# One layer of a hybrid encoder on one core: tiles scaled as rows before they are turned, roots spread later, gains fetched as rows, row tiles stored ahead of h rows

## The chip, the core and the metric

The kernel is one program on one core of a Trainium2 chip. The metric is the time on the device in microseconds (us); the median of three runs of the kernel before is 2344.55 us (2340.38 to 2346.22). The engines are TensorE (PE in the profile), VectorE (DVE), ScalarE (ACT), GpSimd (POOL) and SyncE (SP). SP and GpSimd issue nearly all transfers, and each issues in program order: a transfer whose condition is not met holds up all that stand behind it on that engine.

## The reference

One step of a layer on 1024 prompt tokens and 32 sample tokens, all in fp32. What matters here:

```python
n = rmsnorm(h, g_in)            # x * rsqrt(mean(x*x) + eps) * g_in, per token
z = n @ w_in                    # 2048 -> 6152: q, k, v, f, gates, u
att = forgetting_attention(q, k, v, f)
ssm = s5(u)                     # diagonal state space, GELU, GLU
mixed = concat(att * silu(ga), ssm * silu(gs))
h = h + mixed @ w_out           # the residual is the input x
e = rmsnorm(pe @ w_pe, g_pe)
h = h + e * sigmoid(h @ w_pg)
y = rmsnorm(h, g_final)
```

The outputs are y, k, v, the log of the forget gates and the last states, for prompt and sample.

## The kernel before, in words

Activations are held transposed, features on the 128 partitions and the 1056 tokens along the free axis. The three large products (`w_in`, `w_out`, `w_pg`) are made by a seven-product scheme (Winograd's form of Strassen's): features and tokens are cut in halves, giving seven "sides" (sums and differences of quarter blocks of the activations) and seven weight factors. Each fp32 operand is split into a high and a low part, so a product of one side is 4 feature tiles x 3 combinations x 2 token quarters = 24 matmuls of 264 columns. A *pair* `p` is 256 output columns in one half of the sum; its seven products `r` = 0 to 6 go to three pairs of PSUM banks (X, B, Y). ScalarE makes the high part of each weight factor (`high`) and copies banks, DVE makes the factor sums and low parts (`sums`, `low`) and adds partial results. All engines follow the same double loop, `p` and slot `j`, written out by hand: what stands in slot `j` of a pair on DVE or ScalarE runs in that order and waits on semaphores.

`stage_front` (L196) begins with a prologue. For each of ten token tiles (two halves of 4 x 128 + 16 tokens) SP loads `x_in` (rows of 2048). ScalarE squares and sums the row (`square`), takes the root (`root`) and, after PE has turned the first 1024 features (`turn_x`), copies the turned tile over the first half of `x_in` (`copy_x`), from where SP stores it to `xT` in DRAM, for the residual. DVE makes the reciprocal and a diagonal matrix `x_dg` of it (`spread`); PE multiplies that by ones (L711), which lays the reciprocals of the tile's tokens on every partition; DVE copies them to `rstd_bc` and multiplies the eight turned feature tiles by gain and reciprocal into `n_raw` (`normalize`, L1216). After tile 5's root the first two sides are cast and subtracted (`high_side`, `low_side`); for tiles 5 to 9 DVE also makes four differences (`sub_tiles`). The gain comes by columns, `g_col`, one element per descriptor. The other 1024 features follow during pairs 0 to 5 (`turn_xb`, `copy_xb`, `ride`) and read `rstd_bc`.

`stage_attention` and `stage_side` are not touched. `stage_mix` (L2592) has four groups of eight pairs (`NPM` = 8): pairs 0 to 7 and 8 to 15 for `w_out`, 16 to 23 and 24 to 31 for `w_pg`. Between groups all seven sides are replaced: GpSimd reloads each (`reload_side`), ScalarE casts it, DVE subtracts. Four of the seven sides are made ahead from row tiles, the *ride*: GpSimd loads a ride tile (`load_ride`), DVE makes four differences in slot 6 (`subtract_rides`), GpSimd stores them to `tS` (`store_ride`) and, once all have landed, loads the next tile. The ride for group 2 runs in pairs 11 to 15, beside the part loads (`load_part`) and the stores of h rows (`store_h`) of pairs 8 to 15. SP loads weights, the residual (`load_residual`, into `x_res`), and in pairs 2 to 6 (`E_AT`) one block of e each, which DVE scales in slot 5 by `g_pe` and the reciprocals (`scale_e`, L3242) and SP stores back. In slot 6 follows `c12` (L3227), for which PE's product 1 of the next pair waits.

GpSimd's order in pairs 8 to 15 is this:

```python
for n in range(4):
    if NPM + KEPT <= p + 1 < 2 * NPM and n < 3:
        load_part(p + 1, n)
    if p > NPM:
        store_h(p - 1, n)
if 1 <= r <= NRIDE:
    store_ride(2, r - 1)
if 0 <= r < NRIDE:
    load_ride(2, r)
```

## Time and profile before

| | |
|---|---|
| runs | 2344.55 us median (2340.38 to 2346.22, n = 3) |
| profiled execution | 2348.45 us; its span, first to last instruction, 2346.6 us |
| busy, share of the span | PE 92%, DVE 71%, ACT 43%, POOL 13% |
| mean granted TensorE clock | 0.966 of full speed |
| DMA | 477.63 MB, mean 204 GB/s |
| stretches (us from the start) | prologue to 62.8, rest of the front stage to about 1066, attention to about 1460, side stage to about 1582, mixing stage to the end |

All times in rows are from the start of the span. "Idle before" is how long the engine stood ahead of an instruction, and after the arrow is what ended it. A row with xN is N instructions in one stretch. SPq and POOL rows of DMA are the issue of a transfer, not its landing.

### The profile page before, as it was taken

The page shows a single profiled execution, that of the slowest core. Times are in us where ns is not written, and L with a number is a line of the kernel's source. Part 1 is how long each engine was busy: PE and PEld are TensorE (multiplying, and loading weights), DVE is VectorE, ACT ScalarE, POOL GpSimd, SP SyncE. Part 2 cuts the span into 40 slices and gives each one's busy share as a digit, 9 for nine tenths or more (in the row PEclk, how much of TensorE's full clock was granted, in tenths as well). Part 3 has the DMA queues.
Part 4 walks back from the last instruction along what each step waited for, and adds up shares of the span by engine and source line. Part 5 has one row for each costly group of instructions (what it writes and reads, how often), then busy time and mean ns, then how long its engine had stood idle before and what let it go on. Part 6 is the DMA issues. An engine that isn't in the chain of part 4 may idle for free. (4 is left out here: it accounts for less than half of the span.)

```text
span 2346.6 us, 44727 instructions
## 1 busy us (share of the span) xinstructions
PE 2167.0 (92%) x16739; PEld 2107.7 (90%) x16739; DVE 1656.2 (71%) x3053; ACT 999.1 (43%) x1863; POOL 307.5 (13%) x459
## 2 busy tenths in 40 slices
PE   3999999999999999999979988988899998999994
PEld 3999999999999999999958867988899998999994
DVE  6779767767786878787536655758667657658775
ACT  6443333333533333334457645324235324335554
POOL 0021000000101111111144320000101221101000
PEclk7999999999999999999989998999999999999997
DMA  8484444444557787877367735454766677857578
GB/s 249 136 269 119 144 128 138 140 129 145 197 171 226 217 232 219 229 217 207 106 210 237 234 111 218 147 178 175 274 238 228 228 272 253 302 174 253 212 253 326
DMA packets 328006, 477.63 MB, mean 204 GB/s; under 512 B 78912, under 2 KB 250280, under 8 KB 318016
## 3 DMA queue, kind: packets, MB, share of 16 engines
q1 hardware_dynamic: 265072, 290.58, 39.8%
q0 software_dynamic: 36976, 139.52, 17.3%
q10 hardware_dynamic: 25760, 44.87, 5.9%
q8 instruction: 127, 2.08, 0.4%
q14 instruction: 71, 0.58, 0.1%
HBM read 295.99 MB, written 170.22 MB: 199 GB/s over the span
## 5 line engine op out<-in xcount | busy, mean ns | idle before, releaser
L757 PE MATMUL acc<-t_act,w_hi 128*128 128x264 f32 x5376 | 888.1, 287 | 9.2 <-DVE zb L1319 7.3
L757 PEld LDWEIGHTS acc<-t_act,w_hi 128*128 128x128 f32 x5376 | 748.9, 189 | 15.6 <-issue 14.2
L2937 PE MATMUL m_acc<-m_t_act,m_hi 128*128 128x264 f32 x3584 | 597.6, 289 | 38.2 <-DVE m_zb L3227 9.6
L757 PE MATMUL acc<-t_act,w_lo 128*128 128x264 f32 x2688 | 548.5, 286 | 0.0
L2937 PEld LDWEIGHTS m_acc<-m_t_act,m_hi 128*128 128x128 f32 x3584 | 506.2, 192 | 42.6 <-issue 28.3
L757 PEld LDWEIGHTS acc<-t_act,w_lo 128*128 128x128 f32 x2688 | 417.8, 189 | 0.0
L2937 PE MATMUL m_acc<-m_t_act,m_lo 128*128 128x264 f32 x1792 | 369.2, 288 | 0.0
L1312 DVE TENSOR_TENSOR w_lo<-w_raw_f,w_hi 128x512 fp32r<-128x512 f32 x288 | 198.0, 687 | 136.0 <-ACT w_hi L967 135.7
L967 ACT CAST w_hi<-w_raw_f 128x512 fp32r<-128x512 f32 x288 | 177.9, 618 | 268.6 <-PE acc L757 240.1
L2937 PEld LDWEIGHTS m_acc<-m_t_act,m_lo 128*128 128x128 f32 x1792 | 282.1, 192 | 0.0
L2986 ACT CAST m_hi<-m_raw 128x512 fp32r<-128x512 f32 x192 | 118.7, 620 | 166.3 <-PE m_acc L2937 125.4
L3199 DVE TENSOR_TENSOR m_lo<-m_raw,m_hi 128x512 fp32r<-128x512 f32 x192 | 131.8, 687 | 65.8 <-ACT m_hi L2986 65.8
L651 POOL DMA_DIRECT2D zT<-zb x80 | 43.3, 543 | 341.1 <-DVE zb L1328 142.5
L2244 DVE CUSTOM_DVE_ANT_0 prob<-score,negc_bc 128x128 f32<-128x128 f32 (+8 forms) x72 | 53.4, 750 | 30.2 <-PE score L2017 28.9
L1016 ACT COPY zb<-acc 128x528 f32<-128x528 f32 x40 | 24.0, 600 | 116.4 <-PE acc L757 116.4
L2268 DVE TENSOR_TENSOR pt_lo<-turned,pt_hi 128x512 fp32r<-128x512 f32 (+2 forms) x112 | 52.8, 507 | 27.2 <-ACT pt_hi L2160 25.4
L2149 ACT ACTIVATE prob<-prob,stat 128x128 f32<-128x128 f32 (+8 forms) x72 | 56.1, 781 | 21.7 <-DVE stat L2244 14.8
L665 POOL DMA_DIRECT2D zb<-cT x88 | 47.3, 540 | 131.4 <-issue 54.2
L984 ACT COPY acc<-acc 128x528 f32<-128x528 f32 x48 | 28.0, 583 | 67.8 <-PE acc L757 64.0
L640 POOL DMA_DIRECT2D t_act<-tS x7 | 3.7, 534 | 403.0 <-PE acc L757 403.0
L3153 DVE TENSOR_TENSOR m_t_act<-m_t_act 128x2112 fp32r<-128x2112 f32 x23 | 54.1, 2352 | 0.0
L1312 DVE TENSOR_TENSOR w_lo<-s,w_hi 128x512 fp32r<-128x512 f32 x48 | 33.2, 691 | 25.6 <-ACT w_hi L967 25.6
(429 smaller groups left out, 3391.6 us busy)
## 6 DMA issues: line engine op xcount, KB each, us to landing
w_raw_f<-in_w_in_dram SPq DMA_DIRECT2D x96, 512.0 KB, 3.9
cT<-zb SPq DMA_DIRECT2D x22, 1056.0 KB, 4.2
zb<-cT POOLq DMA_DIRECT2D x88, 264.0 KB, 6.2
zT<-zb POOLq DMA_DIRECT2D x80, 264.0 KB, 4.0
m_e_res<-eT SPq DMA_DIRECT2D x16, 1056.0 KB, 9.6
m_raw<-in_w_out_dram SPq DMA_DIRECT2D x32, 512.0 KB, 6.2
m_raw<-in_w_pg_dram SPq DMA_DIRECT2D x32, 512.0 KB, 6.1
cT<-m_zb SPq DMA_DIRECT2D x12, 1056.0 KB, 5.1
```

What stands on the lines that cost most here:

```text
L651: pool.dma_start(d["zT"][row:row + P, tok:tok + HN], zb[b][:, i]).then_inc(z_put[i], 16)
L665: pool.dma_start(zb[b][:, i], d["cT"][p - NP][:, i]).then_inc(z_got[i], 16)
L757: mm = pe.matmul(out[:, c, 0:QN], w[:, k, :], t_act[:, SIDE[r], x, k, c * QN:(c + 1) * QN], start=(opens and k == 0 and m == 0), stop=(k = ...
L967: nc.scalar.copy(w_hi[n % RING_W][:], factor(p, r)).then_inc(hi_done, 1)
L1312: TT_(w_lo[n % RING_W][:], factor(n // 7, n % 7), w_hi[n % RING_W][:].bitcast(F32), ALU.subtract) \
L2149: e = nc.scalar.activation(prob[s % 4][:, col:col + width], prob[s % 4][:, col:col + width], ACT.Exp, scale=-1.0, bias=stat[b][:, n, 0:1], ...
L2244: z = nc.vector.tensor_tensor_reduce(out=prob[s % 4][:, col:col + width], in0=score[b][:, col:col + width], in1=negc[hb][:, row:row + widt ...
L2268: c = nc.vector.tensor_tensor(out, src, hi.bitcast(F32), ALU.subtract)
L2937: mm = pe.matmul(out[:, c, 0:QN], w[:, k, :], t_act[:, MSIDE[r], x, k, c * QN:(c + 1) * QN], start=(opens and k == 0 and m == 0), stop=(k ...
L2986: nc.scalar.copy(w_hi[n % RING_W][:], factor(p, r)).then_inc(hi_done, 1)
L3153: TT_(t_act[:, MSIDE[s], 1], raw, t_act[:, MSIDE[s], 0].bitcast(F32), ALU.subtract) \
L3199: TT_(w_lo[n % RING_W][:], factor(n // 7, n % 7), w_hi[n % RING_W][:].bitcast(F32), ALU.subtract) \
```

## The change

In the prologue DVE scales the first 1024 features of each tile as rows (`scale_rows`, into `x_rows`), PE turns these too (`turn_rows`), and `normalize` multiplies the turned rows from PSUM by the gain in two operations; so `x_dg`, the matrix of ones and the copy per tile go, and the raw tile is still turned and copied for the residual. The reciprocals are laid out for all tokens by ten matmuls within pair 0 (`spread`) and four ScalarE copies (`copy_bc`). A root is taken ahead of the first square. `copy_x` of a tile follows the next tile's root. The cast and subtraction of side 1 go ahead of weight factors 1 and 2. Both gains (`g_in`, `g_pe`) are loaded as 16 rows of 128 and turned by PE; the second in pair 2 of the mixing stage ahead of product 4. The residual blocks of pairs 8 and 9 are loaded in pairs 3 and 5 rather than both in pair 2. GpSimd stores the ride tiles ahead of part loads and h rows, and reloads sides 1 to 3 between the h rows of pair 14.

```diff
@@ stage_front: PE @@
-            def spread(t):
+            def turn_rows(t):
                 rows = TILES[t][1]
-                pe.wait_ge(dg_done, t + 1)
-                if t >= 2:
-                    pe.wait_ge(bc_copied, t - 1)
-                pe.matmul(oth[:, t % 2, 0:rows], ones[0:rows, :], dg[t % 2][0:rows, 0:rows], start=True, stop=True) \
-                    .then_inc(bc_done, 1)
+                pe.wait_ge(rows_scaled, t + 1)
+                for h in range(2):
+                    if t:
+                        pe.wait_ge(n_half, 2 * (t - 1) + h + 1)
+                    for f in range(KQ):
+                        tr = pe.transpose(acc[:, 4 + h, f * P:f * P + rows],
+                                          x_rows[t % 2][0:rows, (h * KQ + f) * P:(h * KQ + f + 1) * P],
+                                          ident[0:rows, 0:rows])
+                    tr.then_inc(rows_turned, 1)
+            def spread(bank, tiles):
+                pe.wait_ge(rstd_done, max(tiles) + 1)
+                for n, t in enumerate(tiles):
+                    rows = TILES[t][1]
+                    mm = pe.matmul(oth[:, bank, n * rows:(n + 1) * rows], stat[0:rows, t, 2:3].to_broadcast([rows, P]),
+                                   ident[0:rows, 0:rows], start=True, stop=True)
+                mm.then_inc(bc_done, 1)
...
+            turn_x(0)
+            pe.wait_ge(g_loaded, 16)
+            pe.transpose(oth[:, 0, 0:KD], rstd_bc[0:KD, 0:P], ident[0:KD, 0:KD]).then_inc(g_turned, 1)
             for t in range(10):
-                turn_x(t)
-                spread(t)
+                if t < 9:
+                    turn_x(t + 1)
+                turn_rows(t)
...
+                    if p == 0 and r == 3:
+                        spread(0, (0, 1, 2, 3))
+                        spread(1, (5, 6, 7, 8))
+                    if p == 0 and r == 5:
+                        pe.wait_ge(bc_copied, 1)
+                        spread(0, (4, 9))
@@ stage_front: ScalarE @@
+            nc.scalar.activation(stat[:, 0, 3:4], eps[:], ACT.Sqrt)
             for t in range(10):
                 square(t)
                 root(t)
-                copy_x(t)
+                if t:
+                    copy_x(t - 1)
...
+            copy_x(9)
+            high(0)
+            act.wait_ge(t_sub, 5)
+            high_side(2, 1, side_raw[1])
+            for n in range(1, RING_W - 1):
                 high(n)
-            for i, s in ((2, 1), (3, 2)):
-                act.wait_ge(t_sub, 5)
-                high_side(i, s, side_raw[s])
+            high_side(3, 2, side_raw[2])
@@ stage_front: DVE @@
-            def spread(t):
+            def scale_rows(t):
                 dve.wait_ge(std_done, t + 1)
                 nc.vector.reciprocal(stat[0:rows, t, 2:3], stat[0:rows, t, 1:2]).then_inc(rstd_done, 1)
                 dve.wait_ge(rstd_done, t + 1)
                 if t >= 2:
-                    dve.wait_ge(bc_done, t - 1)
-                TS(dg[t % 2][0:rows, 0:rows], ident[0:rows, 0:rows], stat[0:rows, t, 2:3], None, ALU.mult) \
-                    .then_inc(dg_done, 1)
+                    dve.wait_ge(rows_turned, 2 * (t - 1))
+                TS(x_rows[t % 2][0:rows], x_in[t][0:rows, 0:D_MODEL // 2], stat[0:rows, t, 2:3], None, ALU.mult) \
+                    .then_inc(rows_scaled, 1)
...
-                for f in range(8):
-                    s = STT(n_raw[:, f // 4, f % 4, tok:tok + rows], x_t[t][:, f, 0:rows], g_col[:, f:f + 1],
-                            rstd_bc[:, tok:tok + rows], ALU.mult, ALU.mult)
-                s.then_inc(n_done, 1)
+                for h in range(2):
+                    dve.wait_ge(rows_turned, 2 * t + h + 1)
+                    TT_(n_raw[:, h, :, tok:tok + rows], acc[:, 4 + h].rearrange("p (f t) -> p f t", f=KQ)[:, :, 0:rows],
+                        g_col[:, h * KQ:(h + 1) * KQ].unsqueeze(2).to_broadcast([P, KQ, rows]), ALU.mult) \
+                        .then_inc(n_half, 1)
@@ stage_mix: SP @@
                 if p == 2:
                     sp.wait_ge(t_ready, 7)
-                    load_residual(NPM)
-                    load_residual(NPM + 1)
-                    with nc.allow_non_contiguous_dma("per-feature columns of the gain"):
-                        sp.dma_start(g_pe[:], d["g_pe"][0].rearrange("(k p) -> p k", p=P)).then_inc(gains_loaded, 16)
+                    sp.dma_start(x_part[0][0:KD, 0:P], d["g_pe"][0].rearrange("(k p) -> k p", p=P)) \
+                        .then_inc(gains_loaded, 16)
+                if p in (3, 5):
+                    load_residual(NPM + (p - 3) // 2)
@@ stage_mix: GpSimd @@
             for p in range(NPM, 2 * NPM):
                 r = p - FIRST_RIDE[2]
+                if 1 <= r <= NRIDE:
+                    store_ride(2, r - 1)
                 if p == 2 * NPM - 1:
                     reload_side(2, 0)
...
                         store_h(p - 1, n)
-                if 1 <= r <= NRIDE:
-                    store_ride(2, r - 1)
+                    if p == 2 * NPM - 1 and n > 0:
+                        reload_side(2, n)
                 if 0 <= r < NRIDE:
                     load_ride(2, r)
-            for s in range(1, 7):
+            for s in range(4, 7):
                 reload_side(2, s)
@@ stage_mix: PE @@
+                    if p == 2 and r == 4:
+                        pe.wait_ge(gains_loaded, 16)
+                        pe.transpose(oth[:, 0, 0:KD], x_part[0][0:KD, 0:P], ident[0:KD, 0:KD]).then_inc(gains_turned, 1)
@@ stage_mix: DVE, scale_e @@
-                dve.wait_ge(gains_loaded, 16)
+                if n == 0:
+                    dve.wait_ge(gains_turned, 1)
+                    link(nc.vector.tensor_copy(g_pe[:], oth[:, 0, 0:KD]))
```

DVE, prologue, tile 6 with the second tile of differences. Before (`x_in_59` is tile 6; the diagonal made in its first two rows is tile 7's):

```order
L1199 RECIPROCAL x_stat<-x_stat 128x1
L1203 TENSOR_SCALAR x_dg_66<-ident,x_stat 128x128
L1209 COPY rstd_bc<-oth 128x128
L1216 SCALAR_TENSOR_TENSOR n_raw<-x_in_59,g_col,rstd_bc 128x128 x8
L1227 TENSOR_TENSOR zb<-n_raw 128x4x128
L1228 TENSOR_TENSOR zb<-n_raw,zb 128x4x128
L1229 TENSOR_TENSOR n_raw<-n_raw 128x4x128
L1230 TENSOR_TENSOR n_raw<-n_raw,zb 128x4x128
```

And now (the first two rows scale tile 7's rows, `x_in_60`):

```order
L1240 RECIPROCAL x_stat<-x_stat 128x1
L1244 TENSOR_SCALAR x_rows_66<-x_in_60,x_stat 128x1024
L1251 TENSOR_TENSOR n_raw<-acc,g_col 128x4x128 x2
L1262 TENSOR_TENSOR zb<-n_raw 128x4x128
L1263 TENSOR_TENSOR zb<-n_raw,zb 128x4x128
L1264 TENSOR_TENSOR n_raw<-n_raw 128x4x128
L1265 TENSOR_TENSOR n_raw<-n_raw,zb 128x4x128
```

Ten operations on 128 tokens and the copy have become one of 1024 and two of 512 elements; the four differences stay.

SP, mixing stage, pair 2 and the start of pair 3. Before:

```order
L2770 DMA cT<-m_zb 128x2112
L2742 DMA m_raw_21072<-in_w_out_dram 128x4x256
L2755 DMA m_x_res<-xT 128x2x1056 x2
L2777 DMA m_g_pe<-in_g_pe_dram 128x16x1
L2758 DMA m_e_res<-eT 128x2x1056
L2742 DMA m_raw_21073<-in_w_out_dram 128x4x256
L2806 DMA eT<-m_e_res 128x2x1056
```

And now, to the e block of pair 3:

```order
L2805 DMA cT<-m_zb 128x2112
L2777 DMA m_raw_21109<-in_w_out_dram 128x4x256
L2809 DMA m_x_part_22080<-in_g_pe_dram 16x128
L2793 DMA m_e_res<-eT 128x2x1056
L2777 DMA m_raw_21110<-in_w_out_dram 128x4x256
L2841 DMA eT<-m_e_res 128x2x1056
L2805 DMA cT<-m_zb 128x2112
L2777 DMA m_raw_21108<-in_w_out_dram 128x4x256
L2790 DMA m_x_res<-xT 128x2x1056
L2793 DMA m_e_res<-eT 128x2x1056
```

The two residuals have left their place ahead of pair 2's e block; one now stands ahead of pair 3's.

GpSimd, end of pair 14 and pair 15, where the sides for group 2 are reloaded. Before:

```order
L2860 DMA m_ride<-hT 128x1056 x2
L2831 DMA m_t_act<-hT 128x4x528
L2840 DMA hT<-m_x_res 128x528 x4
L2867 DMA tS<-m_ride 128x528 x4
L2831 DMA m_t_act<-tS 128x2112 x2
L2831 DMA m_t_act<-hT 128x4x528
L2831 DMA m_t_act<-tS 128x2112
```

And now:

```order
L2895 DMA m_ride<-hT 128x1056 x2
L2902 DMA tS<-m_ride 128x528 x4
L2866 DMA m_t_act<-hT 128x4x528
L2875 DMA hT<-m_x_res 128x528 x2
L2866 DMA m_t_act<-tS 128x2112
L2875 DMA hT<-m_x_res 128x528
L2866 DMA m_t_act<-tS 128x2112
L2875 DMA hT<-m_x_res 128x528
L2866 DMA m_t_act<-hT 128x4x528
```

The last row tiles have moved ahead of the first reload and of the h rows, and the reloads stand between the h rows.

## Rows read from the trace of the kernel before

**Rows 1.** The page, busy time of the engines (share of the span, instructions)

```profile
PE 2167.0 (92%) x16739; PEld 2107.7 (90%) x16739; DVE 1656.2 (71%) x3053; ACT 999.1 (43%) x1863; POOL 307.5 (13%) x459
```

**Rows 2.** Waits of PE: engine, line, for whom, total us, times, longest

```profile
PE m_acc L2937 <- DVE m_zb L3227: 9.6, 1, 9.6
```

**Rows 3.** Timeline, ScalarE, prologue: start us, us, instruction [idle before]

```profile
6.04 1.28 ACT L907 ACT_TABLE_LOAD   x1 [6.04 <-DMA x_in<-in_x_prompt_dram]
...
9.35 1.28 ACT L913 ACT_TABLE_LOAD   x1
...
11.79 1.92 ACT L907 ACTIVATE x_sq<-x_in 128x2048 f32<-128x2048 f32 x1
...
15.11 1.92 ACT L907 ACTIVATE x_sq<-x_in 128x2048 f32<-128x2048 f32 x1
...
30.23 3.95 ACT L933 CAST t_act<-n_raw 128x2112 fp32r<-128x2112 f32 x2
```

**Rows 4.** Timeline, DVE, second half of the prologue

```profile
42.56 0.29 DVE L1203 TENSOR_SCALAR x_dg<-ident,x_stat 128x128 f32<-128x128 f32 x1
...
43.08 2.19 DVE L1216 SCALAR_TENSOR_TENSOR n_raw<-x_in,g_col,rstd_bc 128x128 f32<-128x128 f32 x8
45.30 0.69 DVE L1227 TENSOR_TENSOR zb<-n_raw 128x512 f32<-128x512 f32 x1
...
48.16 0.29 DVE L1203 TENSOR_SCALAR x_dg<-ident,x_stat 128x128 f32<-128x128 f32 x1
```

**Rows 5.** Timeline, PE, prologue and first product

```profile
29.88 1.47 PE L701 MATMUL acc<-ident,x_in 128*128 128x128 f32 x8
...
62.87 0.78 PE L752 MATMUL acc<-t_act,w_hi 128*128 128x264 f32 x2 [8.24 <-issue]
```

**Rows 6.** Groups of DVE instructions by line and shape: count, busy us, mean ns

```profile
L3363 DVE TENSOR_SCALAR m_y_out<-m_y_all,m_rstd 128x2048 f32<-128x2048 f32 x5 | 6.2, 1282 | 0.5 <-DMA m_y_all<-yS 0.5
...
L3153 DVE TENSOR_TENSOR m_t_act<-m_t_act 128x2112 fp32r<-128x2112 f32 x23 | 54.1, 2352 | 0.0
```

**Rows 7.** Timeline, PE, four fp32 matmuls between products

```profile
770.36 1.06 PE L851 MATMUL oth<-u_in,ws_in 128*128 128x132 f32 x8
```

**Rows 8.** Timeline, SP, ScalarE, DVE and PE, mixing stage, pair 2

```profile
1645.40 2.31 SPq L2755 DMA_DIRECT2D m_x_res<-xT  x2
...
1648.33 12.14 SPq L2758 DMA_DIRECT2D m_e_res<-eT  x1
...
1646.63 0.60 ACT L3021 COPY m_zb<-m_acc 128x528 f32<-128x528 f32 x1 [1.81 <-PE m_acc L2937]
...
1651.74 0.69 DVE L3181 TENSOR_TENSOR m_raw<-m_raw,m_raw 128x512 f32<-128x512 f32 x1 [2.74 <-DMA m_raw<-in_w_out_dram]
...
1667.55 2.55 DVE L3242 SCALAR_TENSOR_TENSOR m_e_res<-m_e_res,m_g_pe,e_rstd 128x1056 f32<-128x1056 f32 x2 [12.70 <-DMA m_e_res<-eT]
1670.02 0.70 DVE L3227 TENSOR_TENSOR m_zb<-m_acc,m_zb 128x528 f32<-128x528 f32 x1
...
1670.87 1.22 PE L2937 MATMUL m_acc<-m_t_act,m_hi 128*128 128x264 f32 x4 [9.58 <-DVE m_zb L3227]
```

**Rows 9.** Stretches: busy us (instructions) of PE, PEld, DVE, ACT, POOL, clock, DMA share, GB/s

```profile
1650.00:1655.00 5.00, 5.00 (x43) 5.00 (x42) 3.12 (x5) 1.31 (x3) 0.84 (x2) 1.00 1.04 386
...
1670.00:1675.00 5.00, 4.13 (x19) 4.17 (x20) 4.97 (x8) 0.62 (x1) 0.00 (x0) 0.50 0.55 220
...
1900.00:1950.00 50.00, 45.09 (x359) 43.94 (x358) 34.11 (x53) 15.82 (x25) 13.64 (x25) 1.00 0.81 282
```

**Rows 10.** Timeline, GpSimd and PE, the crossings at pairs 7 and 15

```profile
1789.78 1.22 PE L2937 MATMUL m_acc<-m_t_act,m_hi 128*128 128x264 f32 x4 [3.94 <-DVE m_zb L3206]
...
1928.40 1.14 POOL L2860 DMA_DIRECT2D m_ride<-hT  x2 [8.10 <-DMA tS<-m_ride]
...
1950.30 1.07 POOL L2831 DMA_DIRECT2D m_t_act<-tS  x2 [5.48 <-DMA tS<-m_ride]
...
1961.24 1.22 PE L2937 MATMUL m_acc<-m_t_act,m_hi 128*128 128x264 f32 x4 [6.77 <-issue]
```

More of the change, by code:

```diff
@@ L235, in stage_front @@
         n_raw = place("n_raw", [P, 2, KQ, T])
-        dg = [place(f"x_dg{b}", [P, P]) for b in range(2)]
+        x_rows = [nc.alloc_sbuf_tensor_at(f"x_rows{b}", [P, D_MODEL // 2], F32, offset=ring_at + 4 * D_MODEL + b * 2 * D_MODEL)
+                  for b in range(2)]
         blk = [[n_raw[:, kh, :, th * HN:(th + 1) * HN] for th in range(2)] for kh in range(2)]
@@ L304, in stage_front @@
         consts, g_loaded, arena_open = sem("consts"), sem("g_loaded"), sem("arena_open")
+        g_turned = sem("g_turned")
         x_loaded = [sem(f"x_loaded{t}") for t in range(10)]
-        x_squared, std_done, rstd_done, dg_done, bc_done, bc_copied, x_turned, x_copied, n_done = (
-            sem(n) for n in ("x_squared", "x_std_done", "x_rstd_done", "dg_done", "bc_done", "bc_copied",
-                             "x_turned", "x_copied", "n_done"))
+        x_squared, std_done, rstd_done, rows_scaled, rows_turned, bc_done, bc_copied, x_turned, x_copied, n_half = (
+            sem(n) for n in ("x_squared", "x_std_done", "x_rstd_done", "rows_scaled", "rows_turned", "bc_done",
+                             "bc_copied", "x_turned", "x_copied", "n_half"))
         xT_stored = [sem(f"xT_stored{t}") for t in range(5)]
@@ L717, in turn_xb @@
                     pe.wait_ge(xb_loaded, 16 * sum(len(list(x_pieces(t))) for i in range(m + 1) for t in (i, i + 5)))
+                if m == 0 and h == 0:
+                    pe.wait_ge(bc_copied, 3)
                 if m == 1 and h == 1:
@@ L1146, in extra, with copy_bc @@
                         nc.scalar.activation(sp_part, sp_part, ACT.Ln, bias=ones_col[0:HEADS, :]).then_inc(gate_ln, 1)
+            def copy_bc(n):
+                first, width, bank, at = ((0, 4 * P, 0, 0), (HN, 4 * P, 1, 0), (4 * P, 16, 0, 0), (HN + 4 * P, 16, 0, 16))[n]
+                act.wait_ge(bc_done, min(n, 2) + 1)
+                return nc.scalar.copy(rstd_bc[:, first:first + width], oth[:, bank, at:at + width])
             act.wait_ge(consts, 1)
+            nc.scalar.activation(stat[:, 0, 3:4], eps[:], ACT.Sqrt)
             for t in range(10):
@@ L1151, in _ @@
                 root(t)
-                copy_x(t)
+                if t:
+                    copy_x(t - 1)
                 if t == 5:
-                    act.wait_ge(n_done, 5)
+                    act.wait_ge(n_half, 10)
                     for i, s in enumerate(BUILD[:2]):
                         high_side(i, s, side_raw[s])
-            act.wait_ge(x_turned, 10)
-            for n in range(RING_W - 1):
+            copy_x(9)
[3 more added lines that the diff above has]
+            for n in range(1, RING_W - 1):
                 high(n)
-            for i, s in ((2, 1), (3, 2)):
-                act.wait_ge(t_sub, 5)
-                high_side(i, s, side_raw[s])
+            high_side(3, 2, side_raw[2])
             for p in range(2 * NP):
@@ L1179, in _ @@
                     high(7 * p + j + RING_W - 1)
+                    if p == 0 and j == 3:
+                        copy_bc(0).then_inc(bc_copied, 1)
+                        copy_bc(1).then_inc(bc_copied, 1)
+                    if p == 0 and j == 5:
+                        copy_bc(2)
+                        copy_bc(3).then_inc(bc_copied, 1)
                     if j == 1 and p > NP and is_silu(p - 1):
@@ L1240, in ride @@
                     dve.wait_ge(t_ready, 7)
+                    dve.wait_ge(bc_copied, 3)
                 if m and h == 0:
@@ L1713, in _ @@
             dve.wait_ge(consts, 1)
-            dve.wait_ge(g_loaded, 16)
+            dve.wait_ge(g_turned, 1)
+            link(nc.vector.tensor_copy(g_col[:], oth[:, 0, 0:KD]))
+            scale_rows(0)
             for t in range(5):
-                spread(t)
-                copy_bc(t)
+                scale_rows(t + 1)
                 normalize(t)
-            spread(5)
             for i, s in enumerate(BUILD[:2]):
@@ L1723, in _ @@
                 if t < 9:
-                    spread(t + 1)
-                copy_bc(t)
+                    scale_rows(t + 1)
                 normalize(t)
@@ L1730, in _ @@
             sums(2)
+            low_side(2, 1, side_raw[1])
             low(1)
             low(2)
-            for i, s in ((2, 1), (3, 2)):
-                low_side(i, s, side_raw[s])
+            low_side(3, 2, side_raw[2])
             for p in range(2 * NP):
@@ L2773, in _ @@
                     sp.wait_ge(t_ready, 7)
-                    load_residual(NPM)
-                    load_residual(NPM + 1)
-                    with nc.allow_non_contiguous_dma("per-feature columns of the gain"):
-                        sp.dma_start(g_pe[:], d["g_pe"][0].rearrange("(k p) -> p k", p=P)).then_inc(gains_loaded, 16)
+                    sp.dma_start(x_part[0][0:KD, 0:P], d["g_pe"][0].rearrange("(k p) -> k p", p=P)) \
+                        .then_inc(gains_loaded, 16)
+                if p in (3, 5):
+                    load_residual(NPM + (p - 3) // 2)
                 if p in E_AT:
```

28 lines of the change are left out of this document (11 added, 17 removed).

## Prediction

> **What bounds the kernel now.** I read the page first: TensorE (PE) is busy for 92% of the span [rows 1], so only the places where PE stands still are worth anything. The waits of PE, longest first, name them, and one entry lies in the stage this change edits: 9.6 us for DVE's `m_zb` [rows 2]. The order of time at each place then gives the cause. There are three.
>
> Prologue: PE's first product starts at 62.87 [rows 5], and all before it is preparation. ScalarE starts at 6.04 with a table load, pays a second at 9.35, and then takes one tile per 3.32 us (11.79 to 15.11); the first side is cast at 30.23 [rows 3]. In the second half DVE never rests: one tile takes 5.60 us (42.56 to 48.16), of which the eight `n_raw` operations take 2.22 and the four subtractions after 45.30 take 2.67 [rows 4].
>
> Pair 2 of the mixing stage (A): SP issues two residual blocks at 1645.40, then the gain by columns, and at 1648.33 the e block, whose issue alone lasts 12.14 us. DVE stands at that e block until 1667.55; behind it is the operation at 1670.02 that PE waits for; PE is idle for 9.58 us [rows 8]. The granted clock falls to 0.5, that is 1.2 instead of 2.4 GHz, after this idleness: 19 matmuls in 4.13 us, where a full window has 43 in 5.00 [rows 9].
>
> Pairs 11 to 16 (B): GpSimd sends the row tiles (`tS`) last, then stands at their landing before it loads the next (8.10 us at 1928.40); the sides are reloaded at 1950.30 only, and PE idles 6.77 us until 1961.24 [rows 10]. In 1900 to 1950, before that gap, 4.9 us are lost in small pieces [rows 9].
>
> **Prologue, part by part.** (1) The root's table is loaded while x travels, so the two loads of 1.28 us go: first root at about 8.4 instead of 10.9. (2) DVE scales whole rows: 128x1024 by a per-row scalar. The trace has 128x2048 of that form in 1282 ns [rows 6], so 0.65 us; the two-tensor form of 2,112 elements costs 2352 ns [rows 6], nearly twice as much per element, which would make it 1.1, the upper bound. (3) Eight STTs, one copy and one small scaling (2.22 + 0.32 + 0.20) become that 0.65 and two multiplications of 128x512 from PSUM; the nearest row has 128x528 in 0.70 us (at 1670.02) [rows 8], so 1.35. A second-half tile falls from 5.60 to about 4.85. (4) In the first half ScalarE's 3.32 us bounds: tile 5's root at about 23.9, then the last small tile's turn and multiplication, casts of the first sides from about 24.7 instead of 30.23: 5.5 earlier. (5) PE now turns each tile twice. Eight transposes take 1.92 us at the low clock, and two sets, 3.84, would exceed 3.32; but the set at 29.88 took 1.47 after PE had been busy since 27.27 [rows 5], so PE speeds up when it has this work. I take ScalarE's pace, and keep 2 us for PE's. (6) The casts and subtractions of the first two sides stay as they are; four full tiles save 0.75 each, the small one about 0.9. End of the prologue: 5.5 + 3.0 + 0.9 = 9.4 us earlier. (7) The roots are spread later, between PE-bound products: 8 + 2 fp32 matmuls. Four such of 132 columns show 1.06 us [rows 7], so 2.1, wholly on the path. The cast of side 1 is moved ahead of two weight casts; product 0 at the low clock lasts over 5 us and covers it, so I give it nothing (up to 0.5). The two ScalarE copies of 512 columns lie beside PE. Prologue net **-7.4**, from -4 (row scaling at 1.1, PE's pace) to -10.
>
> **A.** Residual blocks leave pair 2, and 2,048 elements by columns become 16 rows. The e block then has one store and one 512 KB weight block ahead of it rather than two residuals as well, and lands at about 1655; DVE scales it in 2.5 and does PE's operation by 1659, before PE needs it at 1661.3. So 9.58 and the low-clock loss (16 matmuls at 0.12 = 1.9) go: -11.5. Added: PE turns the gain ahead of pair 2's fifth product. Its third ended at 1646.63 (a copy waited for it) [rows 8], so the fifth starts at 1649.5; the rows of the gain stand behind the weight block which DVE gets at 1651.74: a new stop of 2.3 us (0 if the small load slips through, 4 if it is served late). Moved: a residual now stands ahead of the e block in pairs 3 and 5. 1.08 MB at 386 GB/s [rows 9] is 2.8 us later; the scaling and the operation behind it had some 2 us to spare there: 0.6. A: **-8.6**, from -12 to -5.
>
> **B.** Row tiles go ahead of the h rows, so they leave about 5 us earlier per pair, have landed when the next load is due, and the load goes 7 to 8 us earlier; DVE no longer stands at the ride. Most of the 4.9 goes: -4. At the crossing (pair 15) the last tiles leave near 1932 instead of 1942.7, and the reload of side 1 can go near 1939.5 instead of 1950.30. What is late next is DVE: seven side subtractions of 2.35 each [rows 6] on top of its usual work. The sister crossing at pair 7 has no late reload, and still shows 3.94 us at 1789.78 [rows 10] and the low clock behind it. So 6.77 becomes about 3.9, the restart stays half: -4.5. Side 0 now waits behind the four stores (6 us later), which its first use can just stand. B: **-8.5**; if the reloads simply fill the DMA engines -2, if the whole gap and clock loss go -14.
>
> Sum: 7.4 + 8.6 + 8.5 = 24.5. The profiled execution took 2348.45 (span 2346.6 and 1.85 around it), so 2324.0 for it; it lies 3.9 above the median of the runs, 2344.55, so **2320.0** as a median. Nothing else moves: stages between are shifted as a whole.
>
> **Rivals.** (R1) *The crossing does not improve* (0.17): side 0 is late behind the tile stores and DVE is the bound anyway; B gives 2 instead of 8.5: 2326.5. For it: the sister crossing. Against: 6.77 was a wait for landing, not for DVE.
> (R2) *DVE still stands at the e block* (0.10): with residuals ahead in pairs 3 and 5 it is late there, 3 us each with the operation behind it, and PE waits for the gain's rows: A gives 2.5: 2326.1. Against: pair 5 has no ride traffic.
> (R3) *Dearer table loads* (0.05): each load costs ScalarE a further emptying about as long as itself, so that two removed loads give 2.7 more and all first-half tiles shift: 2317.3. The row at 9.35 shows the next operation at once after 1.28, which speaks against it. The Trainium skill (ScalarE: Activation LUTs, What ACT_TABLE_LOAD costs) puts a drain of about 1.38 us beside the 1.28; the trace has no such gap ahead of the load.
> (R4) *The other side* (0.04): in pairs 12 to 15 GpSimd now stands at DVE's ride result first, with four part loads and four h stores queued behind; SP waits for the landing of all h rows before it loads a residual, and the next weight block queues behind it. It decides once h rows land more than about 8 us later; to lose the other gains each of four pairs must lose some 8 us: 4 x 8 - 16 = 16 slower: 2360. DVE had its result while GpSimd still held other work in every pair seen, hence the small chance.
> (R5) *No change* (0.05): the gains stand, but the freed transfers and the two extra residual slots return all but 4 us as small weight waits: 2341.
>
> **Numbers.** Forecast 0.59, R1 0.17, R2 0.10, R3 0.05, R4 0.04, R5 0.05. About 0.3% (7 us) is what a measurement can tell from no change. Faster by more: 0.59 + 0.17 + 0.10 + 0.05 = 0.91; same 0.05; slower 0.04. Worst ends together (4 + 5 + 2 = 11) give 2333.5, best (10 + 12 + 14 = 36) give 2308.5; both ends together are rare, and runs spread by some 3. Range 2309 to 2333.
>
> **What would show it.** Prologue: one table load before x lands, first product at 53 to 54, a DVE period near 4.9 in the second half, one stop or slow piece of 2 us in the first pair. A: a PE stop of about 2 us ahead of pair 2's fifth product for the gain, none of 9.6, granted clock 1.0 through the pair. B: no GpSimd wait for tile stores ahead of a ride load, side 1 reloaded within 11 us of pair 15's start, a gap of 3 to 5 us. It is wrong if the first product starts after 58, if DVE still waits over 5 us for an e block, or if the crossing keeps 6 us.

## The result and the profile after

The changed kernel takes 2323.79 us, median of 4 runs (2321.29 to 2324.04), against 2345.07 (2340.38 to 2346.22) for the kernel before, run beside it: a ratio of 0.9911, 95% interval 0.9893 to 0.9928. It is 21 us faster; 2320.0 was forecast, with a range of 2309 to 2333. The profiled execution took 2323.73, with a span of 2322.0 (before: 2346.6), so the two traces differ by 24.6 us, while the medians differ by 21.3: the traced execution of before lay 3.4 above its median. The page's first part, TensorE (PE) against [rows 1]:

```profile
PE 2167.6 (93%) x16821; PEld 2109.9 (91%) x16821; DVE 1650.5 (71%) x2985; ACT 1000.7 (43%) x1867; POOL 308.2 (13%) x458
```

The prologue, timeline of ScalarE (start, duration, in brackets the idle time before and what ended it), against [rows 3]:

```profile
0.87 1.28 ACT L1181 ACT_TABLE_LOAD   x1 [0.87 <-PEq L3504]
...
8.26 1.91 ACT L932 ACTIVATE x_sq<-x_in 128x2048 f32<-128x2048 f32 x1 [0.17 <-DMA x_in<-in_x_prompt_dram]
...
11.44 1.92 ACT L932 ACTIVATE x_sq<-x_in 128x2048 f32<-128x2048 f32 x1
...
24.60 3.94 ACT L959 CAST t_act<-n_raw 128x2112 fp32r<-128x2112 f32 x2 [1.07 <-DVE n_raw L1251]
```

One table load, before x is there; a tile every 3.18 us; the first sides are cast at 24.60 instead of 30.23, after a wait of 1.07 us for DVE. The second half on DVE, against [rows 4], has a period of 4.85:

```profile
31.32 0.76 DVE L1244 TENSOR_SCALAR x_rows<-x_in,x_stat 128x1024 f32<-128x1024 f32 x1
31.99 1.28 DVE L1251 TENSOR_TENSOR n_raw<-acc,g_col 128x512 f32<-128x512 f32 x2
...
36.17 0.75 DVE L1244 TENSOR_SCALAR x_rows<-x_in,x_stat 128x1024 f32<-128x1024 f32 x1
```

PE's first product, against 62.87 [rows 5], and the two root spreads that now stand between products:

```profile
53.14 0.78 PE L767 MATMUL acc<-t_act,w_hi 128*128 128x264 f32 x2 [4.71 <-issue]
...
63.58 1.95 PE L723 MATMUL oth<-ident,x_stat 128*128 128x128 f32 x16
...
71.33 0.61 PE L723 MATMUL oth<-ident,x_stat 16*128 16x16 f32 x4
```

Pair 2 of the mixing stage, timeline of SP's queue, PE and DVE, against [rows 8]:

```profile
1637.22 1.01 SPq L2809 DMA_DIRECT2D m_x_part<-in_g_pe_dram  x1
1638.60 0.76 SPq L2793 DMA_DIRECT2D m_e_res<-eT  x1
...
1643.53 0.29 PE L3003 MATMUL m_oth<-ident,m_x_part 16*128 16x16 f32 x1 [2.19 <-DMA m_x_part<-in_g_pe_dram]
...
1650.32 2.55 DVE L3284 SCALAR_TENSOR_TENSOR m_e_res<-m_e_res,m_g_pe,e_rstd 128x1056 f32<-128x1056 f32 x2
```

The e block's issue takes 0.76 us instead of 12.14 and DVE finds it landed, so the old stop of 9.58 us is gone. In its place PE stands 2.19 us for 16 rows of gain. Pair 3, which now has a residual block ahead of the e block:

```profile
1661.70 1.02 SPq L2790 DMA_DIRECT2D m_x_res<-xT  x1
1662.77 1.18 SPq L2793 DMA_DIRECT2D m_e_res<-eT  x1
...
1676.43 2.55 DVE L3284 SCALAR_TENSOR_TENSOR m_e_res<-m_e_res,m_g_pe,e_rstd 128x1056 f32<-128x1056 f32 x2 [5.74 <-DMA m_e_res<-eT]
...
1679.75 0.74 PE L2974 MATMUL m_acc<-m_t_act,m_hi 128*128 128x264 f32 x4 [2.29 <-DVE m_zb L3267]
```

DVE stands 5.74 us there, PE 2.29. What both stops did to the clock stands in the stretches (busy time and matmuls of PE, granted clock, DMA share, GB/s), against [rows 9]:

```profile
1640.00:1645.00 5.00, 2.81 (x17) 0.83 1.00 309
1645.00:1650.00 5.00, 5.00 (x36) 0.83 0.96 367
1650.00:1655.00 5.00, 5.00 (x43) 1.00 0.77 284
...
1675.00:1680.00 5.00, 2.71 (x23) 1.00 0.87 315
1680.00:1685.00 5.00, 5.00 (x31) 0.66 0.59 237
```

Pairs 13 to 16, GpSimd, then PE at the crossing, against [rows 10]:

```profile
1874.27 2.16 POOL L2902 DMA_DIRECT2D tS<-m_ride  x4 [13.81 <-DVE m_ride L3201]
...
1880.70 1.07 POOL L2895 DMA_DIRECT2D m_ride<-hT  x2
...
1922.82 0.54 POOL L2866 DMA_DIRECT2D m_t_act<-tS  x1 [1.55 <-issue]
...
1934.25 0.72 PE L2974 MATMUL m_acc<-m_t_act,m_hi 128*128 128x264 f32 x4 [0.94 <-issue]
1938.91 0.72 PE L2974 MATMUL m_acc<-m_t_act,m_hi 128*128 128x264 f32 x4 [1.51 <-issue]
1943.05 0.73 PE L2974 MATMUL m_acc<-m_t_act,m_hi 128*128 128x264 f32 x4 [0.98 <-DVE m_t_act L3193]
1947.18 0.72 PE L2974 MATMUL m_acc<-m_t_act,m_hi 128*128 128x264 f32 x4 [0.98 <-DVE m_t_act L3193]
```

The row tiles leave first, the next rows are loaded with no wait for their landing, side 1 is reloaded at 1922.82 instead of 1950.30, and the gap of 6.77 has become four of 0.94 to 1.51, 4.41 in all, at full clock.

**Where the time went.** In each pair ScalarE copies a seed from PSUM (`acc<-acc` in the first stage, `m_acc<-m_acc` in the mixing stage). The start of that copy in the kernel before minus its start in another kernel is the lead at that pair. The table has the lead at pair 1 of the first stage and at pair 0 of the mixing stage, what the lead gains in stretches of the mixing stage, and the lead at its last pair. In the column from pair 3 to 4 the kernel before had its long stop; from 2 to 3 lies the stop for the gain, from 4 to 5 the one for the e block of pair 3.

| kernel | first stage, pair 1 | mixing, pair 0 | 2 to 3 | 3 to 4 | 4 to 5 | 5 to 13 | 13 to 17 | 17 to 20 | last pair |
|---|---|---|---|---|---|---|---|---|---|
| the change | 9.6 | 8.2 | -3.9 | +12.2 | -4.0 | -0.3 | +10.2 | +2.4 | 24.7 |
| front_only | 8.3 | 7.5 | 0.0 | +2.0 | 0.0 | -0.2 | -0.3 | +2.7 | 11.8 |
| mix_only | 0.0 | 0.6 | -6.5 | +12.1 | -1.3 | -1.1 | +11.8 | +3.4 | 19.0 |
| pool_undone | 9.0 | 12.6 | -2.6 | +12.1 | -4.0 | -0.6 | -2.6 | +2.9 | 17.9 |
| res_back | 9.1 | 5.5 | -12.4 | +12.1 | 0.0 | +1.3 | +9.9 | +2.8 | 19.2 |
| gain_early | 8.4 | 6.2 | -0.3 | +12.2 | -2.5 | +0.2 | +8.8 | +2.8 | 27.4 |
| res_behind | 8.5 | 6.1 | -4.1 | +12.1 | 0.0 | -0.8 | +9.6 | +2.5 | 25.5 |
| both | 8.9 | 10.5 | -0.3 | +12.2 | +0.1 | +1.3 | +10.4 | +3.0 | 37.3 |
| best | 9.1 | 9.8 | -0.3 | +12.2 | +0.1 | -0.2 | +10.0 | +3.3 | 34.9 |
| best2 | 11.4 | 12.0 | -0.3 | +12.2 | +0.1 | 0.0 | +9.2 | +2.3 | 35.6 |
| no_root_ahead | 6.3 | 5.8 | -2.6 | +12.2 | -4.0 | +2.0 | +10.0 | +2.3 | 25.8 |
| gain_columns | 8.7 | 8.0 | 0.0 | +10.5 | -4.6 | -0.7 | +10.1 | +3.5 | 26.8 |
| stores_only | 9.6 | 7.8 | -2.5 | +12.2 | -2.6 | +0.3 | +7.1 | +2.5 | 24.8 |

Three columns warn the reader. From 17 to 20 every kernel gains some 2.7 us, front_only too, whose mixing stage is that of before: there the one traced execution of before lost time that belongs to no edit. From 3 to 4 front_only gains 2.0, again with no edit there: the old stop lasted 7.32 us in it and 9.58 in the trace of before. PE in front_only:

```profile
1661.03 1.22 PE L2972 MATMUL m_acc<-m_t_act,m_hi 128*128 128x264 f32 x4 [7.32 <-DVE m_zb L3262]
```

So the old stop is worth 12.2 against the one execution and 10.2 against the other. And nine of these kernels (the change, front_only, pool_undone, res_back, gain_early, res_behind, both, gain_columns, stores_only) have the same instructions up to the mixing stage, yet come to it with leads from 5.5 to 12.6. So one execution against another is good to some 3 us either way as a whole. Within one stretch the reading is good to a few tenths where PE never stands; where it has a stop, kernels with the same instructions there still differ: from 2 to 3 the stop for the gain costs from 2.5 (stores_only) to 6.5 (mix_only), though neither has another edit in these pairs.

### The profile page after: what moved, and what is told of

It is laid out like the page before. It is cut to its first block and busy times, and to the rows that moved or that the text cites. A ratio compares the mean times of both kernels' runs of the same rounds, so it can differ in the third digit from the quotient of the medians.

```text
span 2322.0 us, 44822 instructions
## 1 busy us (share of the span) xinstructions
PE 2167.6 (93%) x16821; PEld 2109.9 (91%) x16821; DVE 1650.5 (71%) x2985; ACT 1000.7 (43%) x1867; POOL 308.2 (13%) x458
## 5 line engine op out<-in xcount | busy, mean ns | idle before, releaser
L772 PEld LDWEIGHTS acc<-t_act,w_hi 128*128 128x128 f32 x5376 | 748.3, 189 | 15.4 <-issue 14.1
L2303 DVE TENSOR_TENSOR pt_lo<-turned,pt_hi 128x512 fp32r<-128x512 f32 (+2 forms) x112 | 52.8, 507 | 27.6 <-ACT pt_hi L2195 25.8
L1381 DVE TENSOR_TENSOR zb<-acc,zb 128x528 f32<-128x528 f32 x44 | 31.0, 704 | 29.4 <-PE acc L772 29.4
```

What stands on the lines that cost most here:

```text
L772: mm = pe.matmul(out[:, c, 0:QN], w[:, k, :], t_act[:, SIDE[r], x, k, c * QN:(c + 1) * QN], start=(opens and k == 0 and m == 0), stop=(k = ...
L2303: c = nc.vector.tensor_tensor(out, src, hi.bitcast(F32), ALU.subtract)
```

## The experiments

Twelve kernels ran, each beside the kernel before. All edits are to the changed kernel unless another is named. Each run stands with its median, its ratio to the kernel before and the 95% interval.

### The two halves apart: front_only and mix_only

```
front_only:  stage_front of the change, all after it as before
mix_only:    stage_front as before, all after it of the change
```

> Only the front stage of the change, the mixing stage as before. My theory (the parts add up, each at its own place): the first product starts at 53.1 as in the changed kernel, the spreads in pair 0 and the later stages give 1 to 2 us back, so 8 to 10 us faster than before: 2335 to 2337. The rival (what the prologue saves is lost later, since stages with their own pace or transfers absorb it) gives under 4 us: above 2341. The 9.6 us stop in pair 2 of the mixing stage stays in both.

Measured: 2336.66 us, 0.9966 (0.9955 to 0.9976).

> Only the mixing stage of the change (gain rows, residual blocks later, row tiles first), the front stage as before. Parts add up: about 14.5 us faster than before (16.6 less the 2 that may be this or that), near 2330; of it 4 at pairs 2 to 4, 10 at pairs 14 to 17, 2 at pair 20. Rival (the crossing gained only because the shifted prologue put transfers in another phase): under 8 us, above 2337.

Measured: 2328.50 us, 0.9928 (0.9907 to 0.9949). The two savings, 0.34% and 0.72%, add up to 1.06%, against 0.89% for the whole change (interval 0.72 to 1.07): the halves act independently as far as this can tell, and neither rival held. Against the kernel before beside them, 2344.35, the prologue gives 7.7 us and the rest 15.9. In mix_only PE stood longer for the gain's rows, and from pair 2 to 3 it lost 6.5 where the change lost 3.9:

```profile
1652.21 0.28 PE L2968 MATMUL m_oth<-ident,m_x_part 16*128 16x16 f32 x1 [3.33 <-DMA m_x_part<-in_g_pe_dram]
```

### GpSimd's order undone: pool_undone

```
-    if 1 <= r <= NRIDE:
-        store_ride(2, r - 1)        # ahead of the h rows
...
+    if 1 <= r <= NRIDE:
+        store_ride(2, r - 1)        # behind them, sides 1 to 6 reloaded last
```

> The changed kernel with GpSimd's order of the mixing stage as before (row tiles last, sides reloaded after them). My theory: 10 us at pairs 14 to 17 and 2 at pair 20 come back, 2334 to 2337, with the stop of about 6.8 us ahead of pair 16's second product. Rival (the crossing is bound by DVE's side subtractions, and GpSimd's order moves 3 to 4 us at most): 2327 to 2328.

Measured: 2333.71 us, 0.9957 (0.9938 to 0.9976), so 10 us over the change. Timeline of GpSimd, then of PE:

```profile
1911.84 1.14 POOL L2895 DMA_DIRECT2D m_ride<-hT  x2 [8.81 <-DMA tS<-m_ride]
...
1935.44 1.07 POOL L2866 DMA_DIRECT2D m_t_act<-tS  x2 [6.64 <-DMA tS<-m_ride]
```

```profile
1946.25 1.22 PE L2972 MATMUL m_acc<-m_t_act,m_hi 128*128 128x264 f32 x4 [7.77 <-issue]
```

All three waits of before are back. From pair 13 to 17 the lead moves by -2.6 instead of +10.2: this order is worth 12.8 us in the traces, and 10 by the medians. The 2 us that were expected back at pair 20 did not come: from 17 to 20 this kernel gains 2.9 like all others.

### Only the stores ahead: stores_only

```
-    if p == 2 * NPM - 1 and n > 0:
-        reload_side(2, n)           # between the h rows of pair 14
...
-    for s in range(4, 7):
+    for s in range(1, 7):           # behind them
```

> Edit to the changed kernel: the row tiles still go ahead of the h rows in pairs 11 to 16, but sides 1 to 3 are reloaded after the last h row of pair 15, as before the change. Theory (the part of B at the crossing comes from the earlier reload alone, and the small pieces in 1900 to 1950 from the order of the stores): sides 1 to 3 are reloaded near 1949 instead of 1922.8 to 1933.9, TensorE stops about 6 to 8 us at the crossing with the low clock behind it, the pieces before it stay recovered; 5 to 8 us over the change: median about 2330. Rival (once the row tiles are out early, the order of the reloads is indifferent): level with the change, 2324.

Measured: 2324.54 us, 0.9922 (0.9897 to 0.9946): level with the change. The expectation had the order wrong: sides 1 to 3 go behind the h rows of pair 14, not of 15, and those were ready. GpSimd, then PE:

```profile
1917.71 2.13 POOL L2875 DMA_DIRECT2D hT<-m_x_res  x4
1921.94 1.07 POOL L2866 DMA_DIRECT2D m_t_act<-tS  x2 [2.09 <-DMA tS<-m_ride]
```

```profile
1932.59 0.73 PE L2972 MATMUL m_acc<-m_t_act,m_hi 128*128 128x264 f32 x4 [1.40 <-issue]
1938.87 0.72 PE L2972 MATMUL m_acc<-m_t_act,m_hi 128*128 128x264 f32 x4 [3.12 <-issue]
```

The stretch keeps 7.1 of 10.2 us, with a stop of 3.12 and a lower clock behind it (0.66 in 1940 to 1945). ScalarE stood 3.80 us for side 1 here and 2.18 in the change, so the interleaved reloads may save 3 us. That is not shown: it is one trace, kernels that do interleave them have from 8.8 to 11.8 in this stretch, and the medians are level. Most of the gain comes from the row tiles leaving first.

### The residual blocks back in pair 2: res_back

```
     if p == 2:
         sp.wait_ge(t_ready, 7)
+        load_residual(NPM)
+        load_residual(NPM + 1)
         sp.dma_start(x_part[0][0:KD, 0:P], ...)     # the gain rows
...
-    if p in (3, 5):
-        load_residual(NPM + (p - 3) // 2)
```

> The changed kernel with both residual blocks back ahead of pair 2's e block; the gain still comes as rows. My theory: the 12.7 us wait was made by both, 2,048 single elements and 2 MB of residuals; with the residuals alone the e block is 5 to 6 us later than in the changed kernel, PE stops some 2 us plus the low clock in pair 2, and the 4.0 us that pair 3 loses to the residual ahead of its e block come back: 2322 to 2326, level with the changed kernel. Rival (the residuals alone made the wait): the stop of 9.6 us is back, 2330 or more.

Measured: 2328.85 us, 0.9931 (0.9909 to 0.9952), 5 us over the change, between the two readings. PE:

```profile
1654.45 0.28 PE L3003 MATMUL m_oth<-ident,m_x_part 16*128 16x16 f32 x1 [10.44 <-DMA m_x_part<-in_g_pe_dram]
```

DVE found the e block landed, and in pair 3 the loss of 4.0 was gone, but PE itself stood 10.44 us for 8 KB of gain behind 2 residual blocks. The long stop of before had only changed the engine that meets it. I had weighed the small load by its bytes; issued at 1642.21, it took 12.2 us to land, at 1654.4, and the two residual blocks ahead of it had landed by 1654.2. The Trainium skill (DMA: Bandwidth & Descriptors, Queues, rings and completion order) says that each DMA engine takes the descriptors of one issuer's ring in order; the row agrees, with 10.44 us for 16 short rows.

### Columns or blocks: gain_columns

```
-    sp.dma_start(x_part[0][0:KD, 0:P], d["g_pe"][0].rearrange("(k p) -> k p", p=P))
+    sp.dma_start(g_pe[:], d["g_pe"][0].rearrange("(k p) -> p k", p=P))
...
-    pe.transpose(oth[:, 0, 0:KD], x_part[0][0:KD, 0:P], ident[0:KD, 0:KD])
```

> Edit to the changed kernel: the norm gain of the mixing stage is fetched by columns again (2,048 single elements, no turning by TensorE), while the residual blocks stay in pairs 3 and 5. It tells whether the columns or the residual blocks ahead held the e block in pair 2. Theory (the columns' single elements fill the queues, so that the issue of the e block behind them lasts over 8 us): VectorE stands at the e block of pair 2 until near 1660, TensorE stops 4 to 9 us with the clock loss behind it: median 2325 to 2331. Rival (the residual blocks ahead were the weight): no stop of TensorE over 1 us in pair 2, and with the 3.9 us of the rows' turning gone the median is about 2320.

Measured: 2319.96 us, 0.9894 (0.9876 to 0.9913); in the trace the span is 2320.1. SP's queue and DVE:

```profile
1637.41 1.03 SPq L2810 DMA_DIRECT2D m_g_pe<-in_g_pe_dram  x1
1638.82 4.19 SPq L2793 DMA_DIRECT2D m_e_res<-eT  x1
...
1650.96 2.55 DVE L3279 SCALAR_TENSOR_TENSOR m_e_res<-m_e_res,m_g_pe,e_rstd 128x1056 f32<-128x1056 f32 x2 [4.23 <-DMA m_e_res<-eT]
```

The rival held. The e block's issue behind the single elements lasts 4.19 us, not 12.14; DVE stands at it until 1650.96, and PE stops 0.99 us behind that, with no loss of clock. The traces give the time from the issue of pair 2's e block to its landing:

| ahead of the e block | kernel | us to landing |
|---|---|---|
| gain as rows | the change, pool_undone, stores_only, res_behind | 8.5 to 8.6 |
| gain as rows | mix_only | 9.8 |
| gain by columns | gain_columns | 12.1 |
| two residual blocks, gain as rows | res_back | 14.1 |
| two residual blocks, gain by columns | front_only | 16.9 |
| two residual blocks, gain by columns | before | 19.2 |

Over the 8.6 of the change the columns add 3.5, the residual blocks 5.5 (as expected for res_back), and both together 8.3 to 10.6. So each had a part in the old stop, and the residual blocks the larger one. With them away, fetching this gain as rows costs more (3.9 us from pair 2 to 3) than it saves: from pair 2 to 5 the columns gain 5.9, the rows 4.3.

### The two new stops removed: gain_early, res_behind, both

```
gain_early:  -    if p == 2:                         # the gain rows
             +    if p == 1:
res_behind:  -    if p in (3, 5): load_residual(...)     # ahead of the e block
             +    if p in (3, 5): load_residual(...)     # behind load_w(p + 2, 0)
             +    if p in E_AT: ...
both:        the two together
```

> Edit to the changed kernel: the gain rows are fetched one pair of blocks earlier, in pair 1 of the mixing stage, so that they have landed long before TensorE turns them in pair 2. Theory (the stop for the gain and the clock loss behind it are a cost of their own, 2.2 + 1.7 us): TensorE has no stop at the turning of the gain, the granted clock stays 1.0 through pair 2, pairs 2 to 3 take 3.9 us less, and the loss of 4.0 us at the e block of pair 3 stays: median about 2320, 3.9 under the change. Rival (the stop only hides another lateness, say the e block or the weight blocks of pair 2): a stop of 2 us turns up elsewhere in pairs 2 to 4 and the median stays at 2323 to 2325.

Measured: 2318.69 us, 0.9888 (0.9871 to 0.9904).

> Edit to the changed kernel: the residual blocks of pairs 8 and 9 are still fetched in pairs 3 and 5, but behind the e block instead of ahead of it. Theory (the two residual blocks ahead make the e block of pair 3 late, VectorE stands 5.7 us, TensorE 2.3 us, and the clock loses 1.7 more): the wait at pair 3's e block falls to about 3 us or less, TensorE does not stop there, the clock stays 1.0, 4.0 us less: median about 2320. Rival 1 (the e block is late by its own store and the weight block, as where no residual is fetched): a TensorE stop of over 1 us stays in pair 3, gain under 2 us. Rival 2 (the cost goes to the next weight block, which now stands behind the residuals): a stop on a weight landing in pair 4, no gain.

Measured: 2317.58 us, 0.9883 (0.9866 to 0.9899).

> Both edits at once: gain rows in pair 1, residual blocks behind the e block. Theory: the two losses are independent, 3.9 + 4.0 = 7.9: median about 2316, no TensorE stop over 1 us in pairs 1 to 5 of the mixing stage and a granted clock of 1.0 there. Rival (one lateness runs through both, so that curing one is enough): no more than 4 us below the change, 2320.

Measured: 2312.46 us, 0.9869 (0.9853 to 0.9886). No rival held. The first edit takes the -3.9 away (-0.3 is left), the second the -4.0, where DVE's wait at the e block of pair 3 fell from 5.74 to 1.52 us; together they take 7.9 of the trace, nearly all. Stretches of the run with both, over pairs 2 and 3:

```profile
1640.00:1645.00 5.00, 5.00 (x43) 1.00 1.00 346
1645.00:1650.00 5.00, 5.00 (x43) 1.00 0.81 313
...
1670.00:1675.00 5.00, 5.00 (x44) 1.00 1.03 419
1675.00:1680.00 5.00, 5.00 (x44) 1.00 0.91 343
1680.00:1685.00 5.00, 5.00 (x43) 1.00 1.01 366
```

PE was busy without a break from 1630 to 1690 and the clock stayed at 1.00. By the medians it is 11 us under the change, 3 more than the stops explain, within what identical code shows. The two stops were costs of their own.

### The spreads ahead of product 0: best and best2

```
best:   both, and in the loop over tiles
+    if t == 7: spread(0, (0, 1, 2, 3))
+    if t == 8: spread(1, (5, 6, 7, 8))
        in place of the same two calls in pair 0
best2:  best, and in pair 0
+    load_xb(0)                      # second half of the x rows
     load_w(2, 0)
-    load_xb(0)
```

> Both edits above, and the root spreads done ahead of product 0, while TensorE waits for the last cast, with ScalarE doing the copies of the spread roots there, instead of between TensorE-bound products of pair 0. Theory: the 10 spread matmuls (2.1 us by my forecast) leave the path, the copies fit into ScalarE's idle time, the first product still starts near 53: 2.1 under the run with both edits, about 2314. Rival (the spreads or the copies delay the last cast, or the first pair is bound by something else, its low clock): the first product starts 1 to 2 us later and the median stays at 2316.

Measured: 2313.26 us, 0.9875 (0.9855 to 0.9895). PE:

```profile
53.24 0.78 PE L767 MATMUL acc<-t_act,w_hi 128*128 128x264 f32 x2 [3.86 <-issue]
...
78.32 1.09 PE L739 MATMUL oth<-ident,xb_in 128*128 128x128 f32 x8 [2.31 <-DMA xb_in<-in_x_prompt_dram]
```

The first product starts as before the edit and the 2.56 us of spreads are off the path, but PE then comes 2.31 us too early for the x rows: the lead at pair 1 is 9.1, not 11.4.

> Edit to the run with both edits and the early spreads: in pair 0 of the first stage SP issues the second half of the x rows ahead of the weight block of pair 2 instead of behind it. Theory (the 2.6 us that the early spreads save were given back as 2.3 us of waiting for these x rows at 78.3): the stop at 78.3 goes, about 2.3 us less than the run without this edit, 2.3 under the run with both edits alone: median about 2310. Rival (the x rows land no earlier since they wait for the last built side, or the weight block of pair 2 now stops TensorE): a stop of 1 to 2 us stays or moves into pair 2, median 2312 to 2313.

Measured: 2315.35 us, 0.9880 (0.9862 to 0.9899). SP's queue:

```profile
69.38 0.82 SPq L439 DMA_DIRECT2D xb_in<-in_x_prompt_dram  x2
70.25 9.03 SPq L416 DMA_DIRECT2D w_raw_f<-in_w_in_dram  x2
```

The stop at 78.3 is gone and the lead at pair 1 is 11.4, 2.5 over the run with both, as expected. By the end of the kernel it isn't there: 35.6 against 37.3, lost in small pieces, most of them behind pair 5 of the mixing stage; the median missed the 2310 that was expected. The saving is shown where it is made, not in the kernel's time; both, best and best2 can't be told apart.

### The root's table not loaded ahead: no_root_ahead

```
-    nc.scalar.activation(stat[:, 0, 3:4], eps[:], ACT.Sqrt)
```

> Edit to the changed kernel: the square root is not called on a constant while x travels, so its table is loaded again between the first square and the first root. Theory (a load costs its 1.28 us and no emptying beside it, and ScalarE's pace bounds the first half): every step of the prologue is 1.3 us later (two loads where ScalarE's start was shared), first product at 54.4 to 55.7, median 2325 to 2326.4. Rival (each load brings an emptying of about its own length): 2.7 us or more. Second rival (VectorE bounds the second half whatever ScalarE does): first product still near 53.1, median 2323.8.

Measured: 2322.42 us, 0.9909 (0.9887 to 0.9932). ScalarE:

```profile
5.86 1.28 ACT L932 ACT_TABLE_LOAD   x1 [5.86 <-DMA x_in<-in_x_prompt_dram]
...
9.17 1.28 ACT L938 ACT_TABLE_LOAD   x1
10.47 0.29 ACT L938 ACTIVATE x_stat<-x_stat,eps 128x1 f32<-128x1 f32 x1
...
13.83 1.92 ACT L932 ACTIVATE x_sq<-x_in 128x2048 f32<-128x2048 f32 x1
```

Both loads are back, since the root's table serves the squares too: 2 x 1.28, less the 0.17 that ScalarE waited for x. The third square starts at 13.83 instead of 11.44, 2.39 later, and the first product at 55.51 instead of 53.14, 2.37 later. So the pace of ScalarE carries through to the first product, and a load costs its 1.28 us and nothing beside (9.17 and 1.28 end at 10.45, the root starts at 10.47). The first product lies in the expected 54.4 to 55.7, but the step is 2.39 and not the 1.3 of the theory, since both loads are on the path; both rivals fall. The kernel's median doesn't show it: at 2322.42 it isn't even above the change.

## Why the prediction was right, and where its terms were off

The sum was 24.5 us, and the traces differ by 24.6. Part of that agreement is luck. By the medians the change gives 21.3, 3 less than the sum. The lead in the traces holds 2.4 from pairs 17 to 20, where nothing was changed, and up to 2.0 of the old stop, by which front_only's is cheaper with no edit there. And two terms missed in opposite directions. Of the three signs of being wrong that the prediction names, one came true: DVE did wait over 5 us for an e block, 5.74 in pair 3.

**Prologue, 9.4 at its end and 7.4 net.** Right. The casts came 5.63 earlier (5.5 said), a tile of the second half saves 0.75 (5.60 to 4.85), the first product comes 9.73 earlier. The way to the 5.5 was not quite as told: 3.32 us was the time of one tile of before only, the next two took 3.80 with waits for PE, and in the change tile 5's root starts at 23.03, before the 23.9 of the forecast, whereupon the cast waits for DVE. Of the 9.73 only the 2.39 of the table loads were tested by a run; the rest is read from the rows. The spreads cost 2.56, where 2.1 stood. One gain was not in the sum: PE starts its first product soon after its transposes, and 53 to 58 had a mean clock of 0.69 where the kernel before had 0.50 in the five us from 63; by the first copy the lead was 11.3. Net 9.6 at pair 1, and 8.2 at the mixing stage. front_only alone: 7.7 by the medians.

**The old stop in pair 2, 11.5.** Right: 12.2 against the trace of before, 10.2 against front_only; in gain_columns PE's stop of 0.99 took part of it. The reason was right in kind. I put the e block's lateness on residuals and columns alike; the landing times show that the residual blocks had the larger part (5.5 us alone, the columns 3.5 alone), and res_back that the residual blocks, without columns, hold a load behind them long enough to stop PE for 10.44.

**A, net 8.6.** Wrong by half: 4.3 (12.2 less 3.9 and 4.0), and from 4.3 to 7.1 in the kernels with the same instructions in these pairs, all against the same trace of before. The step that failed is "Added: PE turns the gain", priced as a stop of 2.3, and the one behind it, a residual ahead of the e block at 0.6. The stop for the gain lasted 2.19 as said, but cost 3.9, since the clock fell to 0.83 around it; I had counted on 1.0 through the pair. And the e block of pair 3 held DVE 5.74 us and PE 2.29, where I gave two of 2.8 us to slack that wasn't there: 4.0 instead of 0.6. gain_early, res_behind and both show that the two are independent and together nearly all of what A lacked. The rival that had DVE standing at the e block (R2) was right for pair 3; in pair 5 DVE stood 3.26 us too, as it said, but PE did not stop; its price for A, 2.5, lies nearer to 4.3 than mine does. The total still came out near the forecast because the prologue, B and the pairs from 17 to 20 brought 0.8, 1.7 and 2.4 more than the sum had for them.

**B, 8.5.** Right in kind, low in size: 10.2 in the change, 12.8 against pool_undone. The gap at the crossing fell from 6.77 to 4.41 in four pieces, near the 3.9 I gave it, but in pieces of 0.94 to 1.51 it no longer pulled the clock down, where I had kept half of that loss. I put the gain at the crossing on both the stores and the earlier place of the reloads; stores_only keeps 7.1 with the stores in front alone; whether the place of the reloads makes the other 3 isn't shown. R1, no better crossing, fell by the same rows: the sister crossing was no guide.

**The other rivals.** Dearer table loads (R3): no, 2.39 for two. In the Trainium skill (ScalarE: Activation LUTs, What ACT_TABLE_LOAD costs) the load's 1.28 us agrees with the rows; the drain of about 1.38 that it sets beside it appears in none of them. Slower by waits behind GpSimd's order (R4): GpSimd stood 13.81 us at DVE's ride result, the wait that I had feared, and yet PE was busy without a break from 1875.6 to 1925.6 (411 matmuls in 50 us): what stood behind it on GpSimd was not due. No change (R5): no.

What the interval leaves open: differences under some 3 us between whole kernels, so whether the early spreads and the early root table are worth their 2.4 us in the end. No run takes the row scaling, or the order of the casts, back by itself. Why a stop of one length lowers the clock in one run and not in another wasn't settled either.

## What to carry to other kernels

When a load is made lighter, ask where it lands as well as how long it takes: 8 KB behind two large blocks arrived after them here (res_back), and a consumer on the bounding engine turns a harmless DVE wait into a stop of that engine. Issue such constants a stage early, and put transfers without a near deadline behind the one that is due next. Read the gain of each edit in its own stretch, by the start of one recurring instruction, before the total is believed, and read the same stretch in a second execution of the kernel before: here the old stop lasted 9.58 us in one and 7.32 in the other.
